# A hybrid encoder layer on one core: the second mixer's two time directions in the row halves, tables in four tiles, a new last normalisation

## The chip, the cores and the metric

The kernel runs on one core of a Trainium2 chip. The metric is the device time of one execution in microseconds (us). All data are fp32.

## The reference

One layer of an encoder over 2048 tokens of a sample and 1024 of a prompt, model width 1024: a modulation from a condition, a projection, two mixers side by side (a chunked scan called SSD, and S5), an output product, a layer norm, a routed mixture of 16 experts with the two best per token, and a last layer norm. The parts that the change touches:

```python
def _s5_mixer(u, ...):                       # u: tokens x 512, in 32 groups of 16 channels
    for direction, reverse in ((0, False), (1, True)):
        lam_bar = jnp.exp(lam * step)        # 64 complex states per group
        b_bar = ((lam_bar - 1.0) / lam)[..., None] * b_in
        bu = jnp.einsum('blgi,gpi->blgp', ugc, b_bar)
        _, states = lax.associative_scan(_diag_recurrence, (lam_bar, bu), axis=1, reverse=reverse)
        y = y + jnp.real(jnp.einsum('blgp,gip->blgi', states, c_out))
    y = jax.nn.gelu(y)
...
x = _layer_norm(DEEPNORM_ALPHA * x + g2 * f, ln2_g, ln2_b)     # the last step
```

with `_layer_norm` = (x - mean) * rsqrt(mean((x - mean)^2) + eps) * g + b over the 1024 columns of each row.

## The kernel before

The program is a row of stages, each a block of its own with its own semaphores; a stage starts when the one before has ended on all engines: `modulate`, `project`, `decays`, `scan_back`, `scan_forward` (the SSD mixer), `s5_mixer` (the second mixer), `mix_out`, `route`, `experts`, `combine` (the last normalisation). Within a block each engine has an order written out by hand and waits on counters.

**S5 by chunks.** A chunk is T5 = 16 steps in time; there are C_ALL = 192 chunks (C_S = 128 of the sample, C_P = 64 of the prompt). The 32 groups are taken as 16 pairs; the group in a pair is g, the direction d, real or imaginary r, and k one of the two halves (HALF) of the 16 x 16 = 256 rows of a chunk. Per pair there are tables: w (from a chunk's input to its 64 states), turn (rotations, so that a scan along the chunks needs a real decay only), e (from a chunk's incoming state to its output) and a Toeplitz block toe, made of `kernels`, from the input to the output of one chunk.

**The tables are made in `project`** (L414 on). While PE does the projection's products tile by tile (L571), POOL's `prepare(m)` (L512 to L554) works out pair m: 6 operations for `pre`, 6 for `e`, then a DMA that stores e (L540); 6 for `turn`, two copies (L550), and a DMA that stores it (L552). `pre` of the next pair waits until PE has turned that of this one (w_turned), `e` until PE has used it (kernel_mm). PE has hooks between its tiles, 16 pairs of them: `turn_weights(p)` (L592) transposes `pre`, and `kernel_of(p)` (L596 to L615) multiplies b_bar by e into the first 16 partitions of a PSUM bank per group: 256 columns for direction 0, 16 for the lag zero of direction 1, the diagonal (L613), and 240 columns for the other lags of direction 1. ACT copies both results to SBUF (L675, L683) and stores them.

**`s5_mixer` (L1196 to L1367).** SP loads u (8 DMAs, L1226), and then for each pair w, turn, four pieces of toe and e into one of three slots (L1228 to L1243), each when its last reader has finished. For a pair m:

- DVE `turn_u(m)` transposes u into `ut[:, m % 2]` (L1259); it waits for output(m - 2).
- PE `states(m)` (L1320): 16 matmuls, direction by direction, into the bank `sums[m % 2][d]`, the two groups in the upper and lower 64 partitions.
- DVE `rotate(m)`: four multiplications of the sums by turn, two additions, eight scans (4 for the sample's and 4 for the prompt's chunks, L1287), four multiplications by turn, two operations that write st.
- PE `output(m)`: for the sample and then for the prompt, ut by toe (L1335), and st by e (L1343) with 64 rows for each group; the first st needs rotate(m).
- ACT: gelu into ys and yp (L1361), stored in two halves.

DVE's order is turn_u(m + 1), rotate(m); PE's is states(m + 1), output(m).

**`combine` (L2136 to L2230).** 24 tiles of 128 rows x 1024 in a ring of four. SP loads first ln_g and ln_b as rows copied to all partitions, then v. DVE: mean and variance (bn_stats, L2168, bn_aggr, L2170). POOL: variance + eps (L2191), to the power -1/2 (L2193), minus the mean times that (L2195). ACT: one pass (v - mean) * root (L2219). DVE: by ln_g (L2175). POOL: plus ln_b (L2202). ACT issues the store (L2225).

## Time and profile before

| what | value |
|---|---|
| three runs, median (lowest to highest) | 3703.0 us (3700.46 to 3708.77) |
| the profiled execution, its own time | 3708.0 us |
| its span in the trace | 3706.2 us |
| busy: PE, DVE, ACT, POOL | 3153.6, 1432.8, 540.3, 1210.2 us |
| HBM read, written | 300.0 MB, 136.4 MB |

Busy time is a sum over stages with different limits, so it says little by itself; the rows below go by stage. Times in the trace count from the start of the span. In the trace each fp32 matmul leaves two records, so a count of 16 matmul records is 8 matmuls. DVE, PE, ACT and POOL are the engines that compute; SP here only issues DMAs. "Idle before" names what ended an engine's wait.

### The profile page before, as it was taken

The numbers are of one execution on the slowest core, as the hardware profiler recorded it, in microseconds if no ns is written. First come the engines' busy times: TensorE is split into PE (matmuls) and PEld (weight loads), VectorE is DVE, ScalarE is ACT, GpSimd is POOL, SyncE is SP. The second block draws the span as 40 slices with busy tenths as digits, with TensorE's granted clock in tenths as the row PEclk, the third lists the DMA queues.
The fourth block names the chain that finished last, engine by engine and source line by source line (L and its number), as shares of the span: only waits on it lengthen the run. The fifth ranks groups of instructions, "written<-read, shape, count | busy, mean of one in ns | idle before, by whom it ended". The sixth has DMA issues, their size and how long they took to land. (4 is left out here: it accounts for less than half of the span.)

```text
span 3706.2 us, 33835 instructions
## 1 busy us (share of the span) xinstructions
PE 3153.6 (85%) x10424; PEld 1648.4 (44%) x10425; DVE 1432.8 (39%) x2033; ACT 540.3 (15%) x1058; POOL 1210.2 (33%) x1202
## 2 busy tenths in 40 slices
PE   7999999956787467759999928999999999999940
PEld 3555555532555344525555523444444444444420
DVE  2835423413788545513333361222122221222238
ACT  1112222211232100011111101101101101011012
POOL 0116766712666300002222202223222232222329
PEclk9999999977989777879999969999999999999975
DMA  5122232235222364262222124344454354442235
GB/s 238 74 76 80 99 118 94 82 137 211 66 82 89 94 183 145 77 239 91 97 97 91 53 119 151 102 136 125 130 163 126 113 154 152 117 121 45 56 95 206
DMA packets 131695, 437.62 MB, mean 118 GB/s; under 512 B 16884, under 2 KB 45300, under 8 KB 122644
## 3 DMA queue, kind: packets, MB, share of 16 engines
q1 hardware_dynamic: 86488, 291.18, 22.5%
q0 software_dynamic: 24752, 81.35, 9.2%
q10 hardware_dynamic: 20368, 63.94, 4.5%
q8 instruction: 53, 0.87, 0.1%
q14 instruction: 34, 0.28, 0.0%
HBM read 300.03 MB, written 136.38 MB: 118 GB/s over the span
## 5 line engine op out<-in xcount | busy, mean ns | idle before, releaser
L2008 PE MATMUL bank<-wg,exp_ht 128*128 x1008 | 455.0, 594 | 15.4 <-DVE exp_ht L2091 15.4
L2026 PE MATMUL bank<-wd,exp_hid_t 128*128 x1008 | 442.9, 592 | 0.9 <-ACT exp_hid_t L2062 0.9
L2008 PE MATMUL bank<-wu,exp_ht 128*128 x1008 | 442.9, 592 | 0.0
L1967 POOL DMA_INDIRECT x<-exp_out,exp_rows x63 | 102.6, 1629 | 870.0 <-DVE exp_out L2112 826.1
L2112 DVE TENSOR_TENSOR exp_out<-bank,exp_gates 128x512 f32<-128x512 f32 x126 | 81.2, 686 | 778.1 <-PE bank L2026 778.1
L1550 PE MATMUL bank<-mix_wo,mix_yt 128*128 128x512 f32 x768 | 342.4, 600 | 19.0 <-issue 11.5
L571 PE MATMUL bank<-x_t,w_in 128*128 128x512 f32 x768 | 336.0, 596 | 5.4 <-DVE x_t L481 5.4
L571 PE MATMUL bank<-w_in,x_t 128*128 128x264 f32 (+1 forms) x1152 | 339.6, 455 | 0.0
L2026 PEld LDWEIGHTS bank<-wd,exp_hid_t 128*128 128x128 f32 x1008 | 191.4, 190 | 241.6 <-issue 241.6
L2008 PEld LDWEIGHTS bank<-wu,exp_ht 128*128 128x128 f32 x1008 | 191.5, 190 | 241.1 <-issue 241.1
L2008 PEld LDWEIGHTS bank<-wg,exp_ht 128*128 128x128 f32 x1008 | 188.0, 192 | 227.5 <-issue 227.5
L1955 POOL DMA_INDIRECT exp_h<-h,exp_index x252 | 242.8, 964 | 106.7 <-issue 59.6
L571 PEld LDWEIGHTS bank<-w_in,x_t 128*128 128x128 f32 x1152 | 217.5, 190 | 108.2 <-issue 83.2
L1550 PEld LDWEIGHTS bank<-mix_wo,mix_yt 128*128 128x128 f32 x768 | 143.5, 192 | 188.0 <-issue 176.3
L571 PEld LDWEIGHTS bank<-x_t,w_in 128*128 128x128 f32 x768 | 144.9, 191 | 183.0 <-issue 177.5
L499 DVE SCALAR_TENSOR_TENSOR pro_acc<-pro_raw,pro_cw,pro_acc 128x514 f32<-128x514 f32 x192 | 205.2, 1069 | 6.8
L2062 ACT ACTIVATE exp_hid_t<-bank 128x512 f32<-128x512 f32 x63 | 37.6, 597 | 999.0 <-PE bank L2016 999.0
L497 DVE TENSOR_SCALAR pro_acc<-pro_raw,pro_cw 128x514 f32<-128x514 f32 x48 | 41.6, 867 | 322.4 <-ACT pro_raw L652 322.4
L2098 DVE TENSOR_TENSOR exp_hid<-exp_silu,bank 128x512 f32<-128x512 f32 x63 | 43.3, 688 | 282.0 <-PE bank L2008 282.0
L1343 PE MATMUL bank<-s_e,s_st 64*64 64x256 f32 (+1 forms) x512 | 88.7, 501 | 47.5 <-DVE s_st L1265 47.5
L514 POOL TENSOR_TENSOR pro_work<-pro_work 128x512 f32<-128x512 f32 (+2 forms) x96 | 117.7, 1226 | 7.5
L1446 POOL TENSOR_SCALAR mix_scale<-mix_scale 128x2048 f32<-128x2048 f32 x1 | 2.4, 2392 | 357.2 <-DMA mix_ln_b<-in_ln_b 357.2
(350 smaller groups left out, 3830.2 us busy)
## 6 DMA issues: line engine op xcount, KB each, us to landing
wg<-in_w_gate SPq DMA_DIRECT2D x16, 2048.0 KB, 7.9
wu<-in_w_up SPq DMA_DIRECT2D x16, 2048.0 KB, 9.2
wd<-in_w_down SPq DMA_DIRECT2D x16, 2048.0 KB, 9.2
x_t<-in_x_t SPq DMA_DIRECT2D x6, 2048.0 KB, 9.2
mix_xt<-in_x SPq DMA_DIRECT2D x6, 2048.0 KB
x<-mix_v ACTq DMA_DIRECT2D x24, 512.0 KB, 2.6
h<-mix_h ACTq DMA_DIRECT2D x24, 512.0 KB, 2.7
com_v<-x SPq DMA_DIRECT2D x24, 512.0 KB, 3.9
```

Of the source, the lines that this page charges most:

```text
L497: steps.then(dve.tensor_scalar(to, raw[:, c, 0:SPAN], cw[:, c, 0:1], None, ALU.mult))
L499: steps.then(dve.scalar_tensor_tensor(out=to, in0=raw[:, c, k:k + SPAN], scalar=cw[:, c, k:k + 1], in1=to, op0=ALU.mult, op1=ALU.add))
L514: tt = lambda o, a, b, op: steps.then(pool.tensor_tensor(o, a, b, op))
L571: mul = pe.matmul(bank[n % RING][:, 0:cols], left(k), right(k), start=k == 0, stop=k == KT - 1)
L1343: mul = pe.matmul(to[n][g], st[own, j, r, d, at:at + c], e[own, s, r, d, d * CH5:d * CH5 + TC], start=False, stop=d == 1 and r == 1)
L1550: mul = pe.matmul(C.bank[2 + 2 * (a % 2) + q][:, :], yt[:, j, k, a * P:(a + 1) * P], wo[:, k, q * WIDE:(q + 1) * WIDE], start=k == 0, stop ...
L1955: pool.indirect_dma_start(out=h[:, j, g, :], out_offset=None, in_=h_quads, in_offset=bass.IndirectOffsetOnAxis(ap=index[:, j, g:g + 1], ax ...
L1967: pool.indirect_dma_start(out=y_dram, out_offset=bass.IndirectOffsetOnAxis(ap=rows[:, j:j + 1], axis=0), in_=out[:, j, :], in_offset=None, ...
L2008: mul = pe.matmul(bank[:, :], ht[:, j, k, :], flat(of[:, bass.ds(e % 2, 1), k * DE:(k + 1) * DE]), start=k == 0, stop=k == KT - 1)
L2026: mul = pe.matmul(bank[:, :], hid_t[:, j, k, :], flat(wd[:, bass.ds(e % 2, 1), k * D + q * WIDE:k * D + (q + 1) * WIDE]), start=k == 0, st ...
L2098: dve.tensor_tensor(hid[:], silu[:], up_b[:, :], ALU.mult).then_inc(hid_done, 1)
L2112: dve.tensor_tensor(out[:, j, q * WIDE:(q + 1) * WIDE], bank[:, :], gates[:, j, q * WIDE:(q + 1) * WIDE], ALU.mult).then_inc(out_read, 1)
```

## The change

Three edits go together.

*In the second mixer*, the two directions share a scan. The sums of a group lie in one bank with direction 0 in the upper 64 partitions and direction 1 in the lower 64, whose input chunks are read backwards by PE, so that time runs the same way in both halves. A scan then covers 192 chunks of one group and one of re/im with a decay table that is zero where a sequence ends (turn gets a third part). st is written back in chunk order, direction 1 reversed; since both directions of a group now lie in 128 rows, output needs two matmuls by e per group instead of four with 64 rows. `ut` gets a ring of four, transposed two pairs ahead. The sample's two groups share a PSUM bank, and one gelu takes both. turn and e are loaded in two DMAs each, one for each half of the partitions; output waits for e and st at its start.

*In the projection* e is stored as four tiles and turn as two times three, per group; POOL makes the decay part (one multiplication), a memset and copies for the pads; `kernel_of` puts the 240 columns of direction 1 at partitions 32 to 47, between the matmuls of 256 columns; ACT takes four pieces instead of two and stores them in two DMAs. The table kernels no longer keep direction 1 reversed.

*In `combine`* the ring is six; ACT sums a row (Copy with an accumulator) and the squares of v - mean (Square with an accumulator); POOL does the root alone; DVE does (v - mean) * ln_g and then * root + ln_b, each in one operation. v is loaded ahead of ln_g and ln_b.

```diff
@@ project: prepare
-                    out = e.rearrange("p (r d t i) -> p r d t i", r=2, d=2, t=Q)
+                    out = e.rearrange("p (d r t i) -> p r d t i", r=2, d=2, t=Q)
...
-                    pool.dma_start(e_pack[m], e).then_inc(e_stored, 16)
+                    pool.dma_start(e_pack[m].rearrange("a g n q -> (g n) a q"), e.rearrange("p (a q) -> p a q", a=4)).then_inc(e_stored, 16)
...
+                    steps.done(pool.memset(out[:, 0:2, :, C_P + C_S:C_P + C_S + 1], 0.0))
+                    for to, of in ((1 + C_P + C_S, 1 + C_P), (1, 1 + C_P)):
+                        steps.done(pool.tensor_copy(out[:, 0:2, int(to == 1), to:to + C_P - 1], out[:, 0:2, int(to == 1), of:of + C_P - 1]))
+                    steps.done(pool.tensor_tensor(out[:, 2], unbroken.unsqueeze(1).to_broadcast([P, 2, TURN]),
+                                                  C.decay[:, m * 2:m * 2 + 2].unsqueeze(2).to_broadcast([P, 2, TURN]), ALU.mult))
+                    steps.wait()
                     for d in range(2):
-                        steps.done(pool.tensor_copy(out[:, :, d, 1 + C_S:1 + C_ALL], out[:, :, d, 1 + d * C_P:1 + (d + 1) * C_P]))
-                    steps.wait()
-                    pool.dma_start(turn_pack[m], turn).then_inc(turn_stored, 16)
+                        own = out[:, :, d, C_P * (1 - d):C_P * (1 - d) + C_ALL + 2]
+                        pool.dma_start(turn_pack[m, d].rearrange("a g n c -> (g n) a c"), own).then_inc(turn_stored, 16)
@@ project: kernel_of
-                    part(0, 0, CH5, T5 * CH5, True, False)
-                    part(1, now, 0, CH5, False, False)
+                    for r in range(2):
+                        for g in range(2):
+                            part(r, g, 0, 0, 0, CH5, T5 * CH5, r == 0, False)
+                            part(r, g, 1, AHEAD, now + CH5, CH5, now, r == 0, r == 1)
+                    for r in range(2):
+                        for g in range(2):
+                            part(r, g, 1, 0, now, 0, CH5, False, False)
...
-                    mul = part(1, now + CH5, CH5, now, True, True)
@@ s5_mixer: loads
-                    sp.dma_start(turn[:, s].rearrange("p a d c -> p (a d c)"), turn_pack[m]).then_inc(turn_here[s], 16)
+                    for d in range(2):
+                        sp.dma_start(turn[way[d], s].rearrange("n a g c -> n (a g) c"),
+                                     turn_pack[m, d].rearrange("a g n c -> n (a g) c")).then_inc(turn_here[s], 16)
...
-                    sp.dma_start(e[:, s].rearrange("p r d n -> p (r d n)"), e_pack[m]).then_inc(e_here[s], 16)
+                    for d in range(2):
+                        sp.dma_start(e[way[d], s].rearrange("n r g q -> n (r g) q"),
+                                     e_pack[m, d * 2:d * 2 + 2].rearrange("r g n q -> n (r g) q")[:, :, d * CH5:d * CH5 + TC]).then_inc(e_here[s], 16)
@@ s5_mixer: DVE
-                    if m >= 2:
-                        dve.wait_ge(y_mm, m - 1)
+                    if m >= RING:
+                        dve.wait_ge(y_mm, m - RING + 1)
...
+                    for g in range(2):
+                        for r in range(2):
+                            at = (g * 2 + r) * C_ALL
+                            steps.done(dve.tensor_tensor_scan(z[:, at + 1:at + 1 + C_ALL], turn[:, s, 2, g, 0:C_ALL], x[:, g, r], 0.0,
+                                                              ALU.mult, ALU.add))
...
+                    tt(m1[:], was, by[0], ALU.mult)
+                    tt(m2[:], was[:, :, ::-1, :], by[1], ALU.mult)
...
+                    for d in range(2):
+                        to = st[way[d], j] if d == 0 else st[way[d], j, :, :, ::-1]
+                        tt(to[:, 0], m1[way[d], :, 0], m2[way[d], :, 0], ALU.subtract)
+                        tt(to[:, 1], m1[way[d], :, 1], m2[way[d], :, 1], ALU.add)
...
                 turn_u(0)
+                turn_u(1)
...
-                    if m + 1 < PAIRS:
-                        turn_u(m + 1)
+                    if m + 2 < PAIRS:
+                        turn_u(m + 2)
                     rotate(m)
@@ s5_mixer: PE
+                                for d in range(2):
+                                    seen = ut[:, t, g, k, :] if d == 0 else ut[:, t, g, k, ::-1]
+                                    mul = pe.matmul(sums[j][g][way[d], r * C_ALL:(r + 1) * C_ALL],
+                                                    w[:, s, r, k, d, g * N5:(g + 1) * N5], seen,
                                                     start=k == 0, stop=k == HALF - 1)
...
+                    pe.wait_ge(e_here[s], loads(m) * 2)
+                    pe.wait_ge(rotated, (m + 1) * PER)
...
+                    for g in range(2):
+                        to = of_sample[:, g * TC:(g + 1) * TC]
                         for k in range(HALF):
+                            pe.matmul(to, ut[:, t, g, k, 0:C_S], toe[:, s, g, k, :], start=k == 0, stop=False)
+                        for r in range(2):
+                            pe.matmul(to, st[:, j, r, g, 0:C_S], e[:, s, r, g, :], start=False, stop=r == 1)
@@ combine
+                    act.activation(unused[:, 0, :], v[:, n % RING, :], ACT.Copy, accum_out=one(total, n)).then_inc(summed, 1)
...
+                    act.activation(unused[:, 1, :], v[:, n % RING, :], ACT.Square, bias=one(minus, n), accum_out=one(square, n)).then_inc(squared, 1)
...
+                    pool.tensor_scalar(one(root, n), one(square, n), 1.0 / D, EPS, ALU.mult, ALU.add).then_inc(rooted, 1)
+                    pool.wait_ge(rooted, n * 2 + 1)
+                    pool.tensor_tensor(one(root, n), one(root, n), C.minus_half[:], ALU.pow).then_inc(rooted, 1)
...
+                    dve.scalar_tensor_tensor(out=y[:, r, :], in0=v[:, r, :], scalar=one(minus, n), in1=ln_g[:],
+                                             op0=ALU.add, op1=ALU.mult).then_inc(scaled, 1)
...
+                    dve.scalar_tensor_tensor(out=y[:, r, :], in0=y[:, r, :], scalar=one(root, n), in1=ln_b[:],
+                                             op0=ALU.mult, op1=ALU.add).then_inc(shifted, 1)
```

How the instructions stand on the engines. PE in the second mixer, one pair before (s_ut: the transposed input, s_w, s_toe, s_e: the tables, s_st: the states; a row gives the result's partitions x columns):

```order
L1320 MATMUL bank<-s_ut,s_w 64x192 x16
L1335 MATMUL bank<-s_toe,s_ut 128x256 x4
L1343 MATMUL bank<-s_e,s_st 128x256 x8
L1335 MATMUL bank<-s_toe,s_ut 64x256 x4
L1343 MATMUL bank<-s_e,s_st 64x256 x8
```

and now:

```order
L1340 MATMUL bank<-s_ut,s_w 64x192 x16
L1356 MATMUL bank<-s_toe,s_ut 128x256 x2
L1358 MATMUL bank<-s_e,s_st 128x256 x2
L1356 MATMUL bank<-s_toe,s_ut 128x256 x2
L1358 MATMUL bank<-s_e,s_st 128x256 x2
L1362 MATMUL bank<-s_toe,s_ut 64x256 x4
L1365 MATMUL bank<-s_e,s_st 64x256 x4
```

The sample goes group by group, 24 matmuls of output have become 16, and the wait for st has moved from the first L1343 to the first L1356. DVE in the second mixer, one pair now (s_m, s_x, s_z: the rotation's working tiles):

```order
L1278 STREAM_TRANSPOSE s_ut<-s_us 128x6x2x32 x2
L1284 TENSOR_TENSOR s_m<-bank,s_turn 128x384 x4
L1284 TENSOR_TENSOR s_x<-s_m 128x2x192 x2
L1301 SCALAR_TENSOR_TENSOR s_z<-s_turn,s_x 128x192 x4
L1284 TENSOR_TENSOR s_m<-s_z,s_turn 128x768 x2
L1284 TENSOR_TENSOR s_st<-s_m 64x384 x2
L1284 TENSOR_TENSOR s_st<-s_m 64x2x192 x2
```

Eight scans have become four (L1301), four multiplications of 384 two of 768, and two writes of st four with 64 partitions.

## Rows read from the trace of the kernel before

**Rows 1.** Table by stage: us; PE, PEld, DVE, ACT, POOL busy; clock; DMA; GB/s

```profile
41.90:780.00 738.10, 734.77 (x2646) 408.77 (x2646) 339.03 (x557) 147.79 (x306) 358.15 (x354) 1.00 0.24 93
...
1276.00:1589.60 313.60, 195.05 (x1280) 134.78 (x1280) 144.68 (x353) 22.02 (x65) 0.00 (x0) 0.77 0.51 143
...
3584.40:3706.20 121.80, 0.00 (x0) 0.00 (x0) 100.20 (x96) 29.78 (x24) 101.30 (x96) 0.50 0.60 215
```

**Rows 2.** Timeline, DVE, one pair of the mixer (start, us, engine, line, operation)

```profile
1446.95 1.04 DVE L1259 STREAM_TRANSPOSE s_ut<-s_us 128x384 f32<-128x384 f32 x2 [7.93 <-PE bank L1343]
1447.91 1.91 DVE L1265 TENSOR_TENSOR s_m<-bank,s_turn 128x384 f32<-128x384 f32 x4
1449.85 1.03 DVE L1265 TENSOR_TENSOR s_x<-s_m 128x384 f32<-128x384 f32 x2
1450.80 2.22 DVE L1287 TENSOR_TENSOR_SCAN s_z<-decay,s_x 128x127 f32<-128x127 f32 x8
1453.05 1.96 DVE L1265 TENSOR_TENSOR s_m<-s_z,s_turn 128x384 f32<-128x384 f32 x4
1455.05 1.03 DVE L1265 TENSOR_TENSOR s_st<-s_m 128x384 f32<-128x384 f32 x2
```

**Rows 3.** Timeline, PE, the same pair

```profile
1448.09 2.82 PE L1320 MATMUL bank<-s_ut,s_w 128*64 128x192 f32 x32 [1.19 <-issue]
1450.84 1.99 PE L1335 MATMUL bank<-s_toe,s_ut 128*128 128x256 f32 x8
1456.22 3.78 PE L1343 MATMUL bank<-s_e,s_st 64*128 64x256 f32 x16 [3.39 <-DVE s_st L1265]
1459.93 1.97 PE L1335 MATMUL bank<-s_toe,s_ut 128*64 128x256 f32 x8
1461.84 2.12 PE L1343 MATMUL bank<-s_e,s_st 64*64 64x256 f32 x16
```

**Rows 4.** Timeline, the first st and the mixer's last matmuls

```profile
1323.12 1.03 DVE L1265 TENSOR_TENSOR s_st<-s_m 128x384 f32<-128x384 f32 x2
...
1571.15 1.94 PE L1343 MATMUL bank<-s_e,s_st 64*64 64x256 f32 x16
```

**Rows 5.** Groups by line, DVE, `mix_out`: xcount | busy us, mean ns | idle before

```profile
L1496 DVE SCALAR_TENSOR_TENSOR mix_v<-mix_xt,mix_v 128x1024 f32<-128x1024 f32 x24 | 29.4, 1225 | 0.8
```

**Rows 6.** Table by stretch: with u's load, and with the first store of yg

```profile
1280.00:1310.00 30.00, 0.00 (x0) 0.00 (x0) 0.37 (x1) 0.00 (x0) 0.00 (x0) 0.50 1.03 209
...
1447.00:1464.00 17.00, 12.48 (x80) 8.55 (x80) 8.94 (x22) 1.24 (x4) 0.00 (x0) 0.80 0.89 294
```

**Rows 7.** Timeline, PE, `kernel_of` of one pair, first and last part

```profile
361.80 1.13 PE L605 MATMUL bank<-pro_work,pro_b_bar 64*16 64x256 f32 x16
...
363.01 0.99 PE L605 MATMUL bank<-pro_work,pro_b_bar 64*16 64x240 f32 x8
```

**Rows 8.** Timeline, PE, the modulation's matmuls in four column strips

```profile
24.10 1.92 PE L376 MATMUL bank<-mod_wt,cond 128*32 128x512 f32 x16
```

**Rows 9.** Groups by line, POOL, projection: the store of e

```profile
L540 POOL DMA_DIRECT2D e_pack<-pro_work x15 | 8.7, 578 | 4.5 <-POOL pro_work L514 4.5
```

**Rows 10.** Timeline, POOL: the same store beside DVE's table work

```profile
190.45 0.81 POOL L540 DMA_DIRECT2D e_pack<-pro_work  x1 [0.31 <-POOL pro_work L514]
```

**Rows 11.** Waits, POOL, projection (waiter, releaser, us, times, longest)

```profile
POOL pro_work L519 <- PE bank L592: 133.1, 13, 85.9
POOL pro_work L519 <- issue: 69.4, 7, 9.9
```

**Rows 12.** Groups by line, ACT, last normalisation

```profile
L2219 ACT ACTIVATE com_w<-com_v,com_minus,com_mean 128x1024 f32<-128x1024 f32 x24 | 29.8, 1241 | 101.8 <-POOL com_minus L2195 101.8
```

**Rows 13.** Timeline, PE, forward scan: the first matmuls after two waits

```profile
1068.95 1.31 PE L1055 MATMUL bank<-fwd_skip,ident 128*128 128x512 f32 x2 [2.45 <-DVE fwd_y L1165]
...
1125.27 1.10 PE L1055 MATMUL bank<-fwd_skip,ident 128*128 128x512 f32 x2 [2.44 <-DVE fwd_y L1165]
```

**Rows 14.** Groups of the page: an indirect DMA of 128 rows

```profile
L1967 POOL DMA_INDIRECT x<-exp_out,exp_rows x63 | 102.6, 1629 | 870.0 <-DVE exp_out L2112 826.1
```

More of the change, by code:

```diff
@@ L227, in keep @@
             for c in range(2):
[L228 to L230 removed]
+                steps.then(dve.tensor_copy(to[c][:], power[c].rearrange("p q (a d) -> p a d q", d=2)[:, :, :, 0:n]))
         dve.wait_ge(here, 16 * 10)
@@ L1217, in s5_mixer @@
         sums, yb = (C.bank[0:2], C.bank[2:4]), (C.bank[4:6], C.bank[6:8])
-        segments = ((0, C_S), (C_S, C_P))
+        way = (slice(0, N5), slice(N5, P))
         loads = lambda m: (m // SLOTS + 1) * 16
@@ L1331, in output @@
-                    for n in range(2):
-                        at, c = segments[n]
+                        pe.wait_ge(gelued, (m - 1) * 3)
+                    of_sample, of_prompt = yb[j]
+                    for g in range(2):
+                        to = of_sample[:, g * TC:(g + 1) * TC]
                         for k in range(HALF):
-                            for g in range(2):
-                                pe.matmul(to[n][g], ut[:, j, g, k, at:at + c], toe[:, s, g, k, :], start=k == 0, stop=False)
-                        if n == 0:
-                            pe.wait_ge(e_here[s], loads(m))
-                            pe.wait_ge(rotated, (m + 1) * PER)
-                        for d in range(2):
-                            for r in range(2):
-                                for g in range(2):
-                                    own = slice(g * N5, (g + 1) * N5)
-                                    mul = pe.matmul(to[n][g], st[own, j, r, d, at:at + c], e[own, s, r, d, d * CH5:d * CH5 + TC],
-                                                    start=False, stop=d == 1 and r == 1)
+                            pe.matmul(to, ut[:, t, g, k, 0:C_S], toe[:, s, g, k, :], start=k == 0, stop=False)
+                        for r in range(2):
+                            pe.matmul(to, st[:, j, r, g, 0:C_S], e[:, s, r, g, :], start=False, stop=r == 1)
@@ L1345, in output @@
+                    to = [of_prompt[g * C_P:(g + 1) * C_P, 0:TC] for g in range(2)]
+                    for k in range(HALF):
+                        for g in range(2):
+                            pe.matmul(to[g], ut[:, t, g, k, C_S:C_ALL], toe[:, s, g, k, :], start=k == 0, stop=False)
+                    for r in range(2):
+                        for g in range(2):
+                            mul = pe.matmul(to[g], st[:, j, r, g, C_S:C_ALL], e[:, s, r, g, :], start=False, stop=r == 1)
                     mul.then_inc(y_mm, 1)
```

256 lines of the change are left out of this document (121 added, 135 removed).

## Prediction

> **What bounds the kernel now.** I read the table by stage first, then the timelines of the stages that the change touches. The profiled execution took 3708.0 us (span 3706.2); the median of the runs, 3703.0, lies 5.0 below it. In the projection PE is busy for 734.8 of 738.1 us, in the second mixer for 195 of 313.6, in the last normalisation not at all [rows 1]. The three have three different limits.
>
> In the second mixer the timeline of one pair shows why PE and DVE together stay below full. DVE transposes, rotates, scans and writes st without a pause from 1446.95 to 1456.08, having waited 7.93 us for PE before [rows 2]. PE runs states and the first quarter of output beside that, waits 3.39 us for st, and then works 7.74 us (1456.22 to 1463.96) while DVE stands [rows 3]. DVE's next transpose needs the end of the output before, since `ut` has two buffers: 9.1 + 7.9 us end to end, a period of 17.06 (1446.95 to 1464.01, the start of the next pair). The first st is ready at 1324.15, the last matmul ends at 1573.09 [rows 4].
>
> In the last normalisation POOL is busy for 101.3 and DVE for 100.2 of 121.8 us, ACT for 29.8, and the DMA engines for 0.60 of it [rows 1]: POOL's four operations per tile (101.3 / 24 = 4.2 us) set the pace.
>
> **The mixer's change.** The ring of four lets `turn_u(m + 2)` run when output(m - 2) is done, and states(m + 1) has its input a pair ahead. So DVE and PE run beside each other, and the period is the longer of the two.
>
> DVE, per pair, from [rows 2]: two transposes 0.96 (to the start of the next); four multiplications out of PSUM 1.94, two additions 0.95; now four scans of 192 elements (768) in place of eight (760), at most the 2.25 of before; two multiplications of 768 elements for four of 384, between 1.84 (the 1024-element operation at 1.225 [rows 5], by length) and 2.00, I take 1.9; four writes of st with 64 partitions and 384 elements in place of two with 128. A half-height write costs something between half (1.05 in all) and the same per element (four multiplications of 384: 1.96 [rows 2]); I take the latter, since no row shows that fewer partitions shorten an operation. Sum 0.96 + 1.94 + 0.95 + 2.2 + 1.9 + 2.0 = 9.95 us; bounds 8.8 and 10.1.
>
> PE, per pair: the 16 matmuls of states 2.82 as now [rows 3]; half of them read their input backwards, which no row shows: not below 2.82, above it twice that (5.6). I take 2.82, for the array waits for columns and not for bytes. Output: four matmuls with the whole array now take 1.99 [rows 3]; the sample needs eight such, 3.5 to 4.0; the prompt's eight go in pairs to column halves, four times 0.45 to 0.5: 1.8 to 2.0. Sum 2.8 + 3.5 + 1.8 = 8.1; with every upper end 11.6. DVE at 9.95 is the longer one, with 0.05 for semaphores a period of 10.0.
>
> What could be late next: w, the tables and the kernels come in three slots, and a load is issued when its slot's last reader is done, two periods (20 us) before its use or more. A load now has 512 + 582 + 512 + 512 KiB = 2.17 MB (before 2.00) in packets of 4096, 776, 1024 and 1024 bytes: 217 GB/s at a period of 10. Beside the store of yg the engines moved 294 GB/s at 0.89, mostly in 1 KB packets; with u, at 1.03, 209 [rows 6]. I take 294 as nearer, since three quarters of a load now come in such packets: 7.4 us a load, hidden. SP issues nine DMAs instead of seven per pair; what stands behind each wait in its queue is the next load, with the two periods above to spare.
>
> Start and end: u's arrival sets the start as now. The last two pairs have no transposes: 15 x 10.0 - 2 x 0.96 = 148.1 after 1324.2 the last st is ready, 1472.3; output 5.4 later, 1477.7, against 1573.1. **Mixer: -95 us** (period 9.4 to 11.0: -104 to -80).
>
> **The projection's change.** `kernel_of` runs in PE's full queue: 361.80 to 364.00, 2.2 us a pair, of which the last part (240 columns) is 0.99 [rows 7]. The change puts that part's results at partitions 32 to 47, between the matmuls of 256 columns. Four column strips ran side by side in the modulation: eight matmuls of 512 columns in 1.92 us, where one by one takes 8 x 2 x 0.45 = 7 [rows 8]. Row halves and strips at once aren't shown: between 0 and 0.99 a pair. I take 0.75, nearer to the strips: **-12 us** over 16 pairs. ACT reads four pieces for two and issues one more DMA, under 1 us a pair on an engine that is busy 148 of 738 us.
>
> POOL gets one multiplication of 516 elements (1.3, like its others), a memset, one more DMA issue, and descriptors for 512 and 768 packets instead of 128 and 128. An issue with 128 packets is 0.58 on the mean [rows 9]; if it grows by packets, 4.5 ns each, the pair's 1280 cost 5.8 instead of 1.2. So +2.2 to +6.5 us a pair. POOL's idle time behind PE in this stretch is 133.1 - 85.9 (before the first hook) + 69.4 = 116.6 us over 15 pairs, 7.8 each [rows 11]. That covers it: 0. DVE's four fewer copies of the tables lie before POOL's first work, long ahead of PE's first hook: 0.
>
> **The last normalisation's change.** POOL keeps two operations of one element, DVE does two scalar_tensor_tensor of 1024 (1.225 each [rows 5]) and a small one, 2.6 us; ACT two passes of 1.24 [rows 12], each with a short readout of its accumulator, and a DMA issue: 2.5 to 3.2. The transfers, 1.05 MB a tile: 215 GB/s at 0.60 is 358 at full use [rows 1], 2.9 us. Three limits close together make it somewhat longer than each: 3.0 (2.8 to 3.6). 24 x 3.0 = 72, and about 4 for the first tile (which is now loaded ahead of the two rows of weights), 4 for the last tile's chain of squares, root and shift, 4 for its store: 84 instead of 121.8. **-37 us** (-45 to -24).
>
> Sum: -95 - 12 - 37 = -144, 3564 against the profiled execution, and with its 5 us over the median **3560 us**.
>
> **Rivals.**
>
> *The loads set the mixer's pace.* For it: the 209 GB/s at full use [rows 6], and packets that become smaller. At that rate 16 loads and the first half of yg, 34.7 + 3.1 MB, take 181 us from u's arrival at about 1310 (the end of the first stretch [rows 6]): last output at about 1496, -77 instead of -95: 3577 over the median. Against it: u's transfers fill 32 partitions each, the loads 64 or 128. The Trainium skill (DMA: Bandwidth & Descriptors, "How a descriptor splits into AXI transactions") says that a transfer which doesn't start at a multiple of 256 bytes fetches an extra piece. By it the 776-byte rows take up to 5 pieces instead of 4; as an estimate the tables' 0.60 MB then weigh as 0.75, the 37.8 MB as 40.2, and this rival ends at 3588; no row of before has such a table to test it.
>
> *PE's clock falls in every pair.* Now the granted clock in the mixer is 0.77 on average [rows 1], and after the wait four pairs of matmuls with 256 columns take 3.78, where four before it take 1.99 [rows 3]: the low level. PE would still wait, some 1.8 us a pair. In the forward scan a wait of 2.44 us was followed by a matmul of 1.10 (the high level, 2.4 GHz), one of 2.45 by 1.31 [rows 13]: at 2.4 us it goes either way, at 1.8 more likely not. If 6.8 us of each pair ran at 1.2 GHz, as now (0.80 on average over 17.0 [rows 6]), PE would need 8.1 + 3.4 = 11.5: last output at about 1503, -70, 3584. The Trainium skill (TensorE: Matmul & The Clock Gate, "A second HAM failure mode: psum-queue depth-cycling") tells of just such short stops between groups of matmuls that make the clock swing; by that the rival would be likelier than I give it.
>
> *The two engines still take turns*, through a wait that I have overlooked, or the backward input is slow enough: period 16 to 17, the mixer gains nothing: 3703 - 49 = 3654. Against it: in the order that both engines have, states(m + 1) stands ahead of output(m), and rotate(m + 1) waits for nothing later.
>
> *Slower: POOL's descriptors.* An indirect issue of 128 rows takes 1.63 us [rows 14], 12.7 ns a row; stretched by 1.4, as a direct issue was beside DVE's table work (0.81 [rows 10] against 0.58), it is 17.8 ns. Then a pair's 1280 packets cost 22.8 instead of 1.2, with the new multiplication +23.6; less 7.8 idle, 15.8 x 15 pairs = +237, PE waits at its hooks, and mixer and normalisation give 132 back: 3808. It decides from about 12 ns a packet: 132 / 15 + 7.8 idle - 2.0 for the new work + 1.2 of now = 15.8 us over 1280. Against it: the direct issue's 4.5 ns at most.
>
> **How the numbers follow.** A measurement of this kernel tells 0.2% (7 us) from no change. Forecast 0.62, its own range 3543 to 3588 (period 9.4 to 11, normalisation 2.8 to 3.6 a tile, 0 to 15 from the strips); loads 0.12; clock 0.16; taking turns 0.06; POOL 0.04. Faster in all but the last: 0.95, same 0.02, slower 0.03. The range takes in the forecast, the loads and the clock with somewhat less from the other two terms: 3540 to 3605.
>
> **What would show it.** Right: DVE in the mixer without waits for PE from the second pair on, starts of its transposes 10 us apart; `kernel_of` at 1.3 to 1.5 us; POOL still waiting for PE in the projection; tiles of the last stage 3 us apart. Wrong: SP's or PE's waits on `s_turn` or `s_e` (loads); a granted clock below 0.9 in the mixer (clock); PE waiting for `pro_work` (POOL); a period over 12.

## The result, and the profile after

The changed kernel takes 3577.0 us (median of 4 runs, 3573.0 to 3581.0) against 3704.7: a ratio of 0.9655, 95% interval 0.9639 to 0.9672, 128 us less. The prediction was 3560, with a range from 3540 to 3605. The profiled execution took 3581.0 us (span 3579.3), 4 over the median; the one of before has a span of 3706.2. The two spans differ by 126.9 us. Cut at the same events (the first DMA of u, the last matmul of the mixer, the first DMA of the last stage, the end), they compare like this:

| stretch | before, us | after, us | difference | forecast |
|---|---|---|---|---|
| to the first DMA of u | 1276.1 | 1260.2 | -15.9 | -12 |
| first DMA of u to the last matmul of the mixer | 297.0 | 232.7 | **-64** | **-95** |
| from there to the first DMA of the last stage | 2011.4 | 2012.4 | +1 | 0 |
| last normalisation to the end | 121.8 | 74.0 | **-48** | -37 |

The stages first, cut at the same events as in [rows 1] (projection, mixer, last normalisation; the columns are those given there):

```profile
38.10:764.00 725.90, 720.60 (x2646) 404.96 (x2646) 356.66 (x553) 154.48 (x338) 398.95 (x408) 1.00 0.27 101
1260.20:1509.40 249.20, 151.35 (x1024) 110.51 (x1024) 156.85 (x289) 21.12 (x49) 0.00 (x0) 0.82 0.86 190
3505.20:3579.30 74.10, 0.00 (x0) 0.00 (x0) 59.21 (x72) 54.08 (x96) 52.28 (x48) 0.50 0.91 354
```

In the mixer the DMA share went from 0.51 to 0.86, while DVE is busy for 157 of 249 us and PE for 151: neither of them is the bound. DVE's timeline of one pair, for [rows 2], and PE's, for [rows 3]:

```profile
1367.05 1.04 DVE L1278 STREAM_TRANSPOSE s_ut<-s_us 128x384 f32<-128x384 f32 x2
1371.29 1.95 DVE L1284 TENSOR_TENSOR s_m<-bank,s_turn 128x384 f32<-128x384 f32 x4 [3.20 <-PE bank L1340]
1373.27 1.02 DVE L1284 TENSOR_TENSOR s_x<-s_m 128x384 f32<-128x384 f32 x2
1374.33 1.90 DVE L1301 TENSOR_TENSOR_SCAN s_z<-s_turn,s_x 128x192 f32<-128x192 f32 x4
1376.27 1.83 DVE L1284 TENSOR_TENSOR s_m<-s_z,s_turn 128x768 f32<-128x768 f32 x2
1378.13 2.08 DVE L1284 TENSOR_TENSOR s_st<-s_m 64x384 f32<-64x384 f32 x4
1380.24 1.04 DVE L1278 STREAM_TRANSPOSE s_ut<-s_us 128x384 f32<-128x384 f32 x2
```

```profile
1355.17 2.82 PE L1340 MATMUL bank<-s_ut,s_w 128*64 128x192 f32 x32 [2.53 <-DMA s_w<-w_pack]
...
1366.74 4.50 PE L1340 MATMUL bank<-s_ut,s_w 128*64 128x192 f32 x32 [3.23 <-DMA s_w<-w_pack]
1371.17 1.13 PE L1356 MATMUL bank<-s_toe,s_ut 128*128 128x256 f32 x4
```

DVE's operations are as forecast, but it stands for 3.20 us until the matmuls of states are done, and these had waited 3.23 us for w. The waits of both engines between 1310 and 1480 and what the loads took from issue to landing (the number after the size; before: w 6.5, turn 4.1) say the same:

```profile
DVE s_m L1284 <- PE bank L1340: 28.3, 10, 6.4
```

```profile
PE bank L1340 <- DMA s_w<-w_pack: 33.8, 13, 6.1
```

```profile
s_turn<-turn_pack SPq DMA_DIRECT2D x28, 291.0 KB, 10.5
...
s_w<-w_pack SPq DMA_DIRECT2D x14, 512.0 KB, 11.5
```

Before, SP stood still for most of the mixer until a slot's readers were done, so the loads had time to spare. Now it hardly waits for them: it issues one load after the other, and the DMA engines work nearly without a gap. SP's longest waits between 1300 and 1440, of before and of after:

```profile
SPq L1242 <- PE bank L1343: 47.3, 7, 7.6
SPq L1235 <- DVE s_st L1265: 37.9, 7, 5.7
```

```profile
SPq L1249 <- DVE s_st L1284: 1.4, 4, 0.6
```

And yet the full engines move less. These two stretches of 50 us, of before and of after, hold loads alone, no store of yg:

```profile
1340.00:1390.00 50.00, 36.26 (x250) 25.63 (x248) 26.98 (x66) 3.89 (x12) 0.00 (x0) 0.84 0.42 133
```

```profile
1340.00:1390.00 50.00, 38.72 (x288) 28.24 (x288) 44.89 (x83) 6.20 (x15) 0.00 (x0) 0.97 0.88 190
```

Dividing the rate by the busy share gives the rate at full use: 133 / 0.42 = 317 GB/s before and 190 / 0.88 = 216 after. For the same engine time the loads moved a third less. That is the question of the experiments.

### The profile page after: what moved, and what is told of

It is laid out like the page before. It is cut to its first block and busy times, and to the rows that moved or that the text cites. A ratio compares the mean times of both kernels' runs of the same rounds, so it can differ in the third digit from the quotient of the medians.

```text
span 3579.3 us, 33479 instructions
## 1 busy us (share of the span) xinstructions
PE 3098.8 (87%) x10168; PEld 1624.2 (45%) x10169; DVE 1420.1 (40%) x1941; ACT 570.3 (16%) x1146; POOL 1204.1 (34%) x1208
## 5 line engine op out<-in xcount | busy, mean ns | idle before, releaser
L499 DVE SCALAR_TENSOR_TENSOR pro_acc<-pro_raw,pro_cw,pro_acc 128x514 f32<-128x514 f32 x192 | 225.3, 1174 | 6.8
L1340 PE MATMUL bank<-s_ut,s_w 128*64 128x192 f32 x512 | 59.8, 402 | 86.2 <-DMA s_w<-w_pack 86.2
L1517 DVE TENSOR_TENSOR mix_v<-bank,mix_g 128x512 f32<-128x512 f32 x24 | 16.6, 692 | 235.2 <-PE bank L1574 235.2
```

The source lines that it names most:

```text
L499: steps.then(dve.scalar_tensor_tensor(out=to, in0=raw[:, c, k:k + SPAN], scalar=cw[:, c, k:k + 1], in1=to, op0=ALU.mult, op1=ALU.add))
L1340: mul = pe.matmul(sums[j][g][way[d], r * C_ALL:(r + 1) * C_ALL], w[:, s, r, k, d, g * N5:(g + 1) * N5], seen, start=k == 0, stop=k == HALF ...
```

## The experiments

All are edits of the changed kernel, but for the last. Their readings in one table, from each kernel's own profile: the mixer's stretch as above; the first st after the first DMA of u; the mean period (first to last st, over 15); and the rate at full use between 1340 and 1390 us (GB/s over share). Lower partitions are 0 to 63, where direction 0 lies, and upper ones 64 to 127; the section on the change has these two words the other way round.

| run | median us | ratio to before [95%] | mixer us | first st us | period us | GB/s at full use |
|---|---|---|---|---|---|---|
| before | 3703 to 3709 | 1 | 297.0 | 48.1 | 16.18 | 317 |
| the change | 3577.0 | 0.9655 [0.9639, 0.9672] | 232.7 | 48.3 | 11.73 | 216 |
| tables for 3 pairs | 3555.3 | 0.9589 [0.9573, 0.9605] | 205.5 | 48.1 | 10.00 | none |
| long rows | 3582.9 | 0.9663 [0.9638, 0.9689] | 232.8 | 48.1 | 11.82 | 219 |
| window | 3578.8 | 0.9655 [0.9639, 0.9671] | 223.9 | 49.5 | 11.12 | 209 |
| w by POOL's queue | 3583.4 | 0.9658 [0.9639, 0.9676] | 240.0 | 52.4 | 11.91 | 180 |
| full height | 3550.7 | 0.9588 [0.9568, 0.9608] | 202.8 | 48.4 | 9.79 | 316 |
| two queues | 3580.4 | 0.9660 [0.9638, 0.9682] | 231.2 | 53.2 | 11.37 | 210 |
| u split | 3572.8 | 0.9641 [0.9623, 0.9660] | 219.5 | 38.2 | 11.59 | 214 |
| halves together | 3568.3 | 0.9632 [0.9609, 0.9655] | 213.3 | 37.7 | 11.23 | 194 |
| full, spread | 3549.6 | 0.9567 [0.9550, 0.9583] | 203.4 | 49.0 | 9.79 | 300 |
| half, together | 3581.9 | 0.9664 [0.9648, 0.9680] | 228.5 | 48.1 | 11.53 | 226 |
| full height and u | 3543.6 | 0.9561 [0.9543, 0.9579] | 190.6 | 36.5 | 9.77 | 338 |

The time up to u differs by 15 us between executions (1252.9 to 1268.4 in the runs of the changed kernel's family), whatever was edited behind it. So the mixer's own stretch tells small steps better than the whole time. In the three runs with the shortest mixers the store of yg begins inside the stretch of the last column (at 1378 with full height, 1385 with full, spread, 1371 with full height and u). Between 1330 and 1370, without that store, the rates at full use are 300, 279 and 325 there, 311 before and 215 in the change.

**Are the loads the bound?** Thirteen of the sixteen loads are left out.

```diff
-                for m in range(PAIRS):
+                for m in range(SLOTS):
                     load(m)
...
-        loads = lambda m: (m // SLOTS + 1) * 16
+        loads = lambda m: 16
```

> The changed kernel, whose second mixer loads w, turn, toe and e for the first three pairs only and uses these for all sixteen (13 loads of 2.17 MB are left out, so the values are not the reference's). Loads theory: DVE's 10.0 us of work set the pace, PE no longer holds up DVE, the starts of the transposes lie 10 us apart instead of 11.7, 15 x 1.7 = 26 us less: 3551 us. Clock or turn-taking theory: the pace is set by DVE and PE waiting for each other, the period stays at 11 to 12 us: 3570 to 3577.

Measured: 3555.3, and DVE's starts 9.88 us apart without a wait from the third pair on:

```profile
1343.41 1.04 DVE L1278 STREAM_TRANSPOSE s_ut<-s_us 128x384 f32<-128x384 f32 x2
1353.29 1.04 DVE L1278 STREAM_TRANSPOSE s_ut<-s_us 128x384 f32<-128x384 f32 x2
```

The windows of 100 us from 1330 on (first this run, then the change) show DVE full and TensorE at its upper level throughout, against 0.92:

```profile
1330.00:1430.00 100.00, 83.44 (x664) 64.72 (x662) 98.00 (x182) 13.63 (x33) 0.00 (x0) 1.00 0.11 32
```

```profile
1330.00:1430.00 100.00, 75.70 (x536) 55.94 (x538) 81.04 (x150) 9.92 (x24) 0.00 (x0) 0.92 0.94 218
```

So the loads are the bound. Clock and turn-taking fall: the lower clock of the change is a consequence of PE's waits for w.

**What of the loads? Short pieces, bytes, the queue.** Three edits. In the first the tables are stored with a group's rows together, and loaded so:

```diff
-    turn_pack[m, d].rearrange("a g n c -> n (a g) c")
+    turn_pack[m, d].rearrange("g n a c -> n g (a c)")
-    e_pack[m, d * 2:d * 2 + 2].rearrange("r g n q -> n (r g) q")[:, :, d * CH5:d * CH5 + TC]
+    e_pack[m, d].rearrange("g n r q -> n g (r q)")
```

> The changed kernel with the same bytes in longer pieces: turn_pack and e_pack keep a group's rows together, so a load has 256 pieces of 2328 bytes instead of 768 of 776, and 256 of 2048 instead of 512 of 1024. If the loads' pace comes from short pieces: the DMA engines' rate in the mixer goes back from about 190 to 250 GB/s or more, period 10.0 to 10.5, 3551 to 3560. If it comes from the bytes alone (2.17 MB a pair): no change, 3577. If the loads don't set the pace (clock, turn-taking): no change either, and s_w still lands 11 to 12 us after its issue or sooner, without effect.

Measured: 3582.9 and 232.8 us in the mixer, no change; 219 GB/s at full use. The length of the pieces isn't it.

In the second the two overlapping windows of a kernel row come as one:

```diff
-   for k in range(HALF):
-       rows = bass.AP(tensor=kernels.tensor, offset=(m * 2 + g) * CH5 * LAGS * CH5 + k * SPK * CH5,
-                      ap=[[CH5, SPK], [LAGS * CH5, CH5], [1, TC]])
-       sp.dma_start(toe[:, s, g, k, :], rows).then_inc(toe_here[s], 16)
+   rows = bass.AP(tensor=kernels.tensor, offset=(m * 2 + g) * CH5 * LAGS * CH5,
+                  ap=[[CH5, SPK], [LAGS * CH5, CH5], [1, SPK * CH5 + TC]])
+   sp.dma_start(toe[:, s, g, :], rows).then_inc(toe_here[s], 16)
```

> The changed kernel, in which the two overlapping windows of a kernel row (2 x 1024 bytes) are loaded as one of 1536 bytes: 2.04 instead of 2.17 MB a pair, and 256 pieces of 1536 in place of 512 of 1024. If bytes set the pace: the period goes from 11.7 to 11.0, about -10 us, 3567. If the number of pieces does (1920 to 1664): to 10.2, about -22, 3555. If the loads don't set the pace: 3577.

Measured: 3578.8 in whole, no change that the runs could tell; but the mixer itself takes 223.9 instead of 232.7 and the period is 11.12, near the 11.0 worked out from the bytes. At the same poor rate (209), fewer bytes take less time; the reason for the rate is not touched.

In the third, w goes by another queue:

```diff
-                    sp.dma_start(w[:, s].rearrange("p r k d n -> p (r k d n)"), w_pack[m]).then_inc(w_here[s], 16)
...
+            @block.gpsimd
+            def _(pool):
+                for m in range(PAIRS):
+                    s = m % SLOTS
+                    if m >= SLOTS:
+                        pool.wait_ge(states_mm, m - SLOTS + 1)
+                    pool.dma_start(w[:, s].rearrange("p r k d n -> p (r k d n)"), w_pack[m]).then_inc(w_here[s], 16)
```

> The changed kernel with the mixer's w loaded from POOL's queue instead of SP's; bytes and pieces as before. If one queue's order or its depth holds the loads up (each waits behind those ahead of it in SP's queue): the period falls towards 10.0, down to 3551. If the engines' work holds them up: 3573 to 3581. If the software descriptors of POOL cost more than SP's: slower by up to 10.

Measured: 3583.4 and 240.0 in the mixer; no gain. One queue's depth or order isn't it.

**The height of a transfer.** What is left of the change is that turn and e no longer go to 128 partitions in one DMA, but to 64 and then to the other 64. In [rows 6], u's load, to 32 partitions at a time, ran at 209 GB/s with the engines full. The Trainium skill (SBUF — State Buffer, "Door 1: The DMA port swizzle (why `[64,N]` ≈ `[32,N]`)") says that the lower 64 partitions reach only half of SBUF's sixteen DMA ports, so that 64 are no faster than 32: 196 and 189 GB/s in transfers of 1 MiB, against 328 for all 128. This case agrees: 203 for u between 1270 and 1290 us, against 300 at full use between 1330 and 1370 for loads of full height (the first run below). Two runs are to tell whether height is the cause. In the first, one DMA of full height takes the same bytes from the same queue:

```diff
-   for d in range(2):
-       sp.dma_start(turn[way[d], s].rearrange("n a g c -> n (a g) c"),
-                    turn_pack[m, d].rearrange("a g n c -> n (a g) c")).then_inc(turn_here[s], 16)
+   rows = turn_pack[m].rearrange("d a g n c -> (d a g n) c").rearrange("(p a) c -> p a c", p=P)
+   sp.dma_start(turn[:, s].rearrange("p a g c -> p (a g) c"), rows)
```

(and e in the same way.)

> The changed kernel with turn and e each loaded by one DMA to all 128 partitions in place of two to 64 partitions one after the other; the same bytes, on the same queue, but the rows land in another order, so the values are not the reference's. Half-height theory (a transfer to 32 or 64 partitions goes at about 200 GB/s, one to all 128 at twice that): the transposes start 9.9 to 10.2 us apart, DVE does not wait for PE, 3553 to 3558. If volume or the number of DMAs in one queue holds the loads up: 3573 to 3581.

Measured: 3550.7, period 9.79, mixer 202.8. Between 1340 and 1390 the engines move a third more in a smaller share (some of it the store of yg, from 1378 on), and DVE is full:

```profile
1340.00:1390.00 50.00, 40.85 (x320) 31.59 (x320) 48.97 (x92) 6.21 (x15) 0.00 (x0) 1.00 0.81 256
```

In the second, the halves stay but go by two queues (`turn_half` and `e_half` are the DMAs of one direction; SP issues those of direction 0 where it issued both):

```diff
+                def upper(m):
+                    if m >= SLOTS:
+                        act.wait_ge(rotated, (m - SLOTS + 1) * PER)
+                    turn_half(act, m, 1)
+                    e_half(act, m, 1)
+
+                for m in range(SLOTS):
+                    upper(m)
                 for m in range(PAIRS):
                     of_sample, of_prompt = yb[m % 2]
                     act.wait_ge(y_mm, m + 1)
+                    if m + SLOTS < PAIRS:
+                        upper(m + SLOTS)
```

> The changed kernel with the lower 64 partitions of turn and e loaded by SP as now and the upper 64 by ACT's queue, so that both halves can arrive at the same time; bytes, pieces and heights as before. Half-height theory: as with full height, 3553 to 3560, if the two queues really run beside each other. If a half-height transfer is slow by itself (whatever runs beside it): 3573 to 3581. The run with w on POOL's queue, which gained nothing, stands against a gain from a second queue as such.

Measured: 3580.4, 210 GB/s at full use, no gain. The same page of the Trainium skill ("Can I just issue two DMAs to hit both halves?") says that they can't be fused and only one transfer over all partitions reaches all ports; for turn and e the trace agrees.

The run with full height changed a second thing: its rows also lay together in memory. Two more runs complete the square. Full height, pieces spread:

```diff
+   rows = turn_pack[m].rearrange("d a g n c -> (d a) (g n) c").rearrange("x p c -> p x c")
+   sp.dma_start(turn[:, s].rearrange("p a g c -> p (a g) c"), rows)
```

> The changed kernel with turn and e each loaded by one DMA to all 128 partitions, but with the pieces that a partition gets as far apart in memory as in the changed kernel (776 and 1024 bytes, 99 and 139 KB apart); the rows land in another order, so the values are not the reference's. The run with full height had its pieces together as well, and the run with two queues gained nothing, so two theories are left. Half-height theory: 3545 to 3556, the transposes 9.9 us apart. Scattered-pieces theory (what a partition gets must lie together in memory): 3573 to 3581.

Half height, pieces together:

```diff
+   rows = turn_pack[m].rearrange("d a g n c -> (d a g n) c").rearrange("(p a) c -> p a c", p=P)
+   for d in range(2):
+       sp.dma_start(turn[way[d], s].rearrange("p a g c -> p (a g) c"), rows[way[d]])
```

> The counterpart: turn and e by two DMAs to 64 partitions each, as in the changed kernel, but each partition's pieces together in memory (4656 bytes in one piece for turn, four of 1024 for e at 1088 from start to start); the rows land in another order, so the values are not the reference's. Half-height theory: 3573 to 3581, the engines at about 190 GB/s. Scattered-pieces theory: 3545 to 3556.

Measured: 3549.6 and 3581.9, periods 9.79 and 11.53. The same 50 us, full and spread first:

```profile
1340.00:1390.00 50.00, 41.43 (x325) 32.08 (x324) 49.00 (x92) 6.20 (x15) 0.00 (x0) 1.00 0.79 237
```

```profile
1340.00:1390.00 50.00, 40.85 (x311) 29.85 (x310) 46.07 (x86) 6.20 (x15) 0.00 (x0) 0.97 0.89 201
```

Spread pieces cost a little of the rate (279 against 300 between 1330 and 1370), but no time. Wherever the pieces lie, full height gains 26 and 27 us against the change (30 and 29 in the mixer), and half height gains nothing that the runs could tell (the mixer of the last is 4 us shorter). Full height also means seven DMAs a pair instead of nine, but their number isn't the cause: the run with the window has seven as well and stayed at 209 GB/s. Nor is it SP's time for issuing them: with two queues SP issued two fewer a pair, without a gain. The records of single packets in the traces say the same: turn's packets of 776 bytes took 62 ns on the mean in the change (1320 to 1398 us), which is 201 GB/s over the 16 engines; u's packets come to 197. In the run with full height and spread pieces they took 42 ns (1318 to 1384). Height is the cause.

**u.** It comes by eight DMAs of 32 partitions, before and after the change. Here those of the upper 64 go by ACT's queue:

```diff
-                for q in range(4):
-                    load_u(q)
+                for q in range(2):
+                    load_u(sp, q)
...
+                for q in range(2, 4):
+                    load_u(act, q)
```

> The changed kernel with u's eight DMAs to 32 partitions each (6.3 MB, 31 us at 204 GB/s) split: those of the lower 64 partitions on SP's queue, those of the upper 64 on ACT's. Half-height theory: u arrives up to 15 us sooner; the mixer behind it stays loads-bound, so about 15 us less: 3562. If reading u's memory sets the 204 GB/s: 3577.

Measured: u's rate between 1270 and 1290 goes from 203 (the change) to 323 GB/s, and the first st is 10 us earlier:

```profile
1270.00:1290.00 20.00, 0.00 (x0) 0.00 (x0) 0.00 (x0) 0.00 (x0) 0.00 (x0) 0.50 1.03 203
```

```profile
1270.00:1290.00 20.00, 0.00 (x0) 0.00 (x0) 0.00 (x0) 1.28 (x1) 0.00 (x0) 0.50 1.01 323
```

The mixer is 13 us shorter (219.5), the whole 4. In the profiled execution u began 8 us later, since `modulate`, which is not edited, ended 9 us later. So here two queues do reach both halves, against the section quoted last. Why they do for u and didn't for turn and e, the runs don't settle: with u the same amount stood in both queues at once, while in the run with turn and e SP's queue also carried w and toe, and the two queues waited for different things.

Both edits by halves, with the window (the three diffs above in one kernel):

> The changed kernel with both of these (u, turn and e by halves on two queues) and the window of 1536 bytes for toe: half-height theory: 24 us from the mixer's pace, 15 from u and some 5 from the first tables, which no longer stand behind u: 3530 to 3540, with DVE busy at 98% from the second pair on. Otherwise 3570 to 3581.

Measured: 3568.3, mixer 213.3; the expected 3530 to 3540 missed, since its main part, turn and e by two queues, gains nothing, as the run with two queues shows by itself.

**A version that beats both.** turn_pack and e_pack are stored in the order of the mixer's partitions, by POOL in eight DMAs a pair (shown for turn; e alike; u and the window as above):

```diff
-   pool.dma_start(turn_pack[m, d].rearrange("a g n c -> (g n) a c"), own)
+   for g in range(2):
+       own = out[g * N5:(g + 1) * N5, :, d, C_P * (1 - d):C_P * (1 - d) + C_ALL + 2]
+       pool.dma_start(turn_pack[m, d, :, g], own)
...
+   sp.dma_start(turn[:, s].rearrange("p g a c -> p (g a c)"), turn_pack[m].rearrange("d n g a c -> (d n) (g a c)"))
```

> A version that should beat both kernels with the reference's values: turn_pack and e_pack ordered by partition of the mixer, so that turn and e come by one DMA of full height with a partition's pieces together; u's lower half on SP's queue, its upper on ACT's; toe by a window of 1536 bytes. POOL stores the tables in eight DMAs a pair instead of three (one for each half of its partitions and each direction). Both theories of the loads: 26 us from the mixer's pace as in the run with full height, 10 to 15 from u: 3535 to 3545. If POOL's five further issues (0.8 us each, 4 us a pair) hold up PE in the projection: up to 40 more, 3575 to 3585.

Measured: 3543.6, inside the expected 3535 to 3545; 0.9561 [0.9543, 0.9579] of before, 33 us under the change; mixer 190.6, period 9.77. POOL's further issues found cover: its idle time in the projection shrank, and PE's last hook came 462.5 us after the first as in the change. POOL's waits, in the change and then in this run (84.2 of the 92.4 and all of the 82.7 lie before PE's first hook):

```profile
POOL pro_work L519 <- PE bank L601: 92.4, 8, 84.2
POOL pro_work L519 <- issue: 61.7, 7, 9.0
```

```profile
POOL pro_work L519 <- PE bank L605: 82.7, 1, 82.7
...
POOL pro_work L519 <- issue: 37.9, 7, 8.0
```

**The other two parts alone.** The kernel before with `kernel_of`, `take_kernel` and `combine` of the change, whose diffs stand in the section on the change:

> The kernel before with the change's other two parts only: the kernel tables in four tiles and the new last normalisation; the second mixer and its tables as before. If the parts add up as the profiles show them (16 from the projection, 48 from the last normalisation): 3703 - 64 = 3639, and the mixer's own share of the change is 62 to 64. By the prediction's terms: 3703 - 12 - 37 = 3654.

Measured: 3650.3, 0.9851 [0.9838, 0.9865], some 55 us less than before. In its profile the last stage takes 74.2 us (-47.6, the same), u's first DMA comes 8.1 us sooner, not 16, and the unchanged mixer took 3.0 longer. The last stage alone is thus confirmed. The 16 of the expectation was too much for the projection: some 4 of it stand before it, as its timeline below shows. The mixer's share of the change is 3650.3 - 3577.0 = 73 us by the medians, 64 by the stretch.

## Why the prediction was right, and where it was wrong

The time is inside the range, 17 us above the forecast. The mixer's term was too large by 31 us, the last normalisation's too small by 11, and 4 came from an earlier end of `modulate`, which is not edited. So that the whole comes as near as 17 is partly luck, and the path that the forecast took through the mixer, with DVE as the bound and the loads hidden, is not what happened.

Of the signs that it named, those of being right failed in the mixer: DVE waited for PE, and its transposes lay 11.7 us apart. The loads showed, but in PE's wait for w, which stands in the same queue behind turn and e, and not in waits on `s_turn` or `s_e`. The granted clock of the mixer was below 0.9 (0.82), the sign of the clock rival, and yet the clock didn't set the pace.

**The mixer, -95 forecast, -64 measured.** The failing step is "I take 294 as nearer, since three quarters of a load now come in such packets: 7.4 us a load, hidden." The 294 GB/s of [rows 6] were loads to 128 partitions beside a store; the price of the new loads stood in the other row, u's 209. The sentence that set it aside, "u's transfers fill 32 partitions each, the loads 64 or 128", took 64 for nearer to 128, and 64 behaves like 32 (201 GB/s by turn's packets, 197 by u's). 2.17 MB at the measured 190 GB/s take 11.4 us, longer than DVE's 9.9; the period was 11.73. The rival *the loads set the mixer's pace* names what happened, but blames the packets. Its 181 us from u's arrival at 1310 would have been -77. Counted from that point with u 15.9 sooner, the last matmul came after 199. That its whole, 3577, is the measured time is chance: its mixer is 13 us too short, and the other stages made that good. Its estimate of five pieces for a row of 776 bytes doesn't follow from the rule as quoted: if a table starts at a multiple of 256 bytes, its rows start at most 248 past one, and 248 + 776 = 1024 is the end of the fourth piece. No run here shows a cost of odd starts; fewer, longer pieces changed nothing. With the height restored, the mixer's step is right as a mechanism: period 9.8, DVE without waits for PE, and with it 202.8 instead of 297.0, -94.

DVE's sum was right: 9.95 forecast, 9.88 measured, with scans at 1.91 for 2.2 and the four half-height writes of st at 2.08 for 2.0. A write of 64 partitions took as long as one of 128 with the same columns before (2.08 for four, 1.03 for two [rows 2]). PE's sum was right too: in the run with full height (one pair; start, us) states take 2.77 with half of their inputs read backwards, and output 5.6 (1341.44 to 1347.01) for 5.3:

```profile
1341.44 1.10 PE L1354 MATMUL bank<-s_toe,s_ut 128*128 128x256 f32 x4 [1.71 <-DVE s_st L1282]
...
1345.98 1.03 PE L1363 MATMUL bank<-s_e,s_st 128*64 128x256 f32 x8
1346.84 2.77 PE L1338 MATMUL bank<-s_ut,s_w 128*64 128x192 f32 x32
```

**The clock rival.** Its stop of about 1.8 us a pair is there (1.71), and the granted clock stayed 1.00 in the run with full height (1340 to 1390): it falls. The section that the prediction quoted from the Trainium skill (TensorE: Matmul & The Clock Gate, "A second HAM failure mode: psum-queue depth-cycling") tells of a clock that swings with such stops; here it did not. After longer waits it went either way, as the prediction had read: 2.53 us was followed by states at 2.82, 3.23 by 4.50 (PE's rows above).

**The projection, -12 forecast, -12 measured.** `kernel_of` took 1.29 us instead of 2.2: the last part runs wholly beside the first, where the prediction gave 0.75 of 0.99 [rows 7].

```profile
356.59 1.14 PE L612 MATMUL bank<-pro_work,pro_b_bar 64*16 64x256 f32 x24
357.66 0.22 PE L624 MATMUL bank<-pro_d_diag,ident 16*16 16x16 f32 x4
357.81 0.88 PE L590 MATMUL bank<-ident,pro_out 128*128 128x128 f32 x6
```

The hooks of the first and the last pair (their first transposes, before and then after) lie 475.2 and 462.5 us apart: 12.7 less over 15 pairs. From its first matmul to its last the projection takes 739.1 and 726.8 us, 12.3 less. The other 3.6 of the table's 15.9 lie almost wholly before it: in the execution of after, the projection's first matmul began 3.7 us sooner, behind a `modulate` that is not edited. In the executions of the changed kernel and its variants that matmul begins anywhere between 38.1 and 47.4.

```profile
284.60 1.04 PE L592 MATMUL bank<-ident,pro_work 128*128 128x128 f32 x8
...
759.81 1.04 PE L592 MATMUL bank<-ident,pro_work 128*128 128x128 f32 x8
```

```profile
281.22 1.04 PE L601 MATMUL bank<-ident,pro_work 128*128 128x128 f32 x8
...
743.73 1.04 PE L601 MATMUL bank<-ident,pro_work 128*128 128x128 f32 x8
```

**POOL** was covered as forecast: PE had no idle time before the matmuls that use its tables (the last number of a row: idle time before):

```profile
L612 PE MATMUL bank<-pro_work,pro_b_bar 64*16 64x256 f32 (+2 forms) x384 | 18.2, 306 | 0.0
L601 PE MATMUL bank<-ident,pro_work 128*128 128x128 f32 x128 | 16.6, 273 | 0.0
```

Its two stores of turn take 1.57 us a pair, that of e 0.81; that is far from the 12 ns a packet at which the slower rival decides (1280 packets in 2.4 us, under 2 ns each).

**The last normalisation, -37 forecast, -48 measured.** The step "three limits close together make it somewhat longer than each: 3.0" is mis-sized: a tile takes 2.45 us, DVE's own work without a gap.

```profile
3528.84 1.27 DVE L2244 SCALAR_TENSOR_TENSOR com_y<-com_v,com_minus,com_ln_g 128x1024 f32<-128x1024 f32 x1
3530.04 1.27 DVE L2251 SCALAR_TENSOR_TENSOR com_y<-com_y,com_root,com_ln_b 128x1024 f32<-128x1024 f32 x1
3531.23 0.14 DVE L2237 TENSOR_SCALAR com_minus<-com_total 128x1 f32<-128x1 f32 x1
3531.30 1.27 DVE L2244 SCALAR_TENSOR_TENSOR com_y<-com_v,com_minus,com_ln_g 128x1024 f32<-128x1024 f32 x1
```

The 1.27 of one overlaps the start of the next by 0.07, so a period is less than the durations added. The transfers were mis-sized too: the 358 GB/s that were worked out from share and rate of before are 398 at a share of 1.01 here, so that the DMA engines were as full as DVE:

```profile
3515.00:3565.00 50.00, 0.00 (x0) 0.00 (x0) 48.89 (x61) 47.22 (x85) 43.66 (x40) 0.50 1.01 398
```

24 x 2.45 = 58.8; start and tail are 74.0 - 58.8 = 15.2, for 12, of which DVE waited 3.9 for the row of weights that is loaded behind the first tile:

```profile
3514.06 0.15 DVE L2237 TENSOR_SCALAR com_minus<-com_total 128x1 f32<-128x1 f32 x1 [3.92 <-DMA com_ln_b<-in_ln_b]
```

## What to carry to other kernels

When a change splits a tensor over the two halves of the partitions, look at its transfers as well as at its arithmetic: the packets of a DMA to 64 partitions ran here at the rate of those to 32, and one DMA over all 128, with its rows in the order of the partitions, gave back all that the split had lost. When an estimate has two measured rates to choose from, ask in what the transfers behind them are alike (height, direction, neighbours) before their packet size. And a stage that becomes faster asks for its loads sooner: work out the load's time at the worse rate, and if that is longer than the new period, the load is the forecast.

## What the hardware did that was not expected

- A mixed stream of loads, half of its bytes at half height, ran at 216 GB/s at full use, hardly above u's load alone, to 32 partitions at a time (203 / 1.03 = 197). If each kind kept its own rate, 1.12 MB at 197 and 1.05 at the 317 of before would take 9.0 us and would have been hidden. The records of single packets show that the half-height transfers slow those beside them: w's packets of 4096 bytes, to all 128 partitions, took 257 ns on the mean in the change and 194 in the run with full height and spread pieces. By what they do so, the runs don't show.
- POOL's operations of one element stretch beside DVE's: in the last stage the addition before the root takes 0.19 us while DVE waits and 0.81 in the steady part, the root itself 0.58 and 1.47. The timeline of POOL, the first tile and a later one:

```profile
3512.46 0.19 POOL L2227 TENSOR_SCALAR com_root<-com_square 128x1 f32<-128x1 f32 x1 [19.44 <-ACT com_unused L2204]
3512.73 0.58 POOL L2229 TENSOR_TENSOR com_root<-com_root,minus_half 128x1 f32<-128x1 f32 x1
...
3529.35 0.81 POOL L2227 TENSOR_SCALAR com_root<-com_square 128x1 f32<-128x1 f32 x1
3530.25 1.47 POOL L2229 TENSOR_TENSOR com_root<-com_root,minus_half 128x1 f32<-128x1 f32 x1
```

- Matmuls that use row halves and column strips at once ran fully beside each other: twelve of them (four with 256, four with 240 and four with 16 columns; 24 records) took 1.14 us, where the eight without the 240 columns (16 records) took 1.13 before.
